# A two-block decoder kernel: latent norm summed on TensorE in small pieces, VectorE alone for the projection weights' low parts, rotary halves placed by DMA

## The reference

```python
a = h @ w_dqkv                                  # 1024 -> 384 + 256 + 32
c_q, c_kv, k_rope = split(a, [384, 384 + 256])
c_q, c_kv = rmsnorm(c_q, q_norm), rmsnorm(c_kv, kv_norm)
q = (c_q @ w_uq).reshape(B, L, 16, 96)          # 64 plain + 32 rotary per head
q = concat([q[..., :64], apply_rope(q[..., 64:], cos, sin)])
kv = (c_kv @ w_ukv).reshape(B, L, 16, 64 + 64)
k_nope, v = split(kv, [64])
k = concat([k_nope, broadcast(apply_rope(k_rope), over 16 heads)])
# causal softmax(q k^T * scale) v for each head, then @ w_o
```

## Time and profile before

| | |
|---|---|
| runs | 979.62 us median of 3 (979.53 to 981.09) |
| profiled execution | 979.78 us, of which span 978.0 us |
| PE busy | 922.1 us (94%), 7282 matmuls |
| DVE busy | 689.9 us (71%) |
| ACT busy | 517.0 us (53%) |
| POOL busy | 322.4 us (33%) |
| mean granted TensorE clock | 0.966 of full |
| DMA | 145.65 MB, mean 149 GB/s |

### The profile page before, as it was taken

The page is one execution under the profiler, slowest core; times in us unless marked ns, Lnnn a source line. Parts: engine busy times, 40 slices in busy tenths (PEclk is TensorE's granted clock), DMA queues, the critical chain, the costliest instruction groups (busy, mean ns, idle before and its releaser), DMA issues.

```text
span 978.0 us, 19924 instructions
## 1 busy us (share of the span) xinstructions
PE 922.1 (94%) x7282; PEld 895.4 (92%) x7282; DVE 689.9 (71%) x1176; ACT 517.0 (53%) x851; POOL 322.4 (33%) x225
## 2 busy tenths in 40 slices
PE   6789988999999998899999899899989999999996
PEld 6787778999998997799999899898889999999995
DVE  7457634999998225399999723779777888785666
ACT  5466655566666334656666534463346454454433
POOL 4534755000002553300000355332127334335643
PEclk9799998999999997899999999899999999999998
DMA  7322013344455352135445445253224455455431
GB/s 260 135 86 87 2 44 129 130 175 175 172 183 217 128 192 81 44 130 192 191 174 188 178 178 188 87 207 138 87 92 179 179 197 184 182 211 204 177 129 44
DMA packets 20848, 145.65 MB, mean 149 GB/s; under 512 B 2480, under 2 KB 4032, under 8 KB 5440
## 3 DMA queue, kind: packets, MB, share of 16 engines
q1 hardware_dynamic: 20800, 144.99, 40.2%
HBM read 143.94 MB, written 1.05 MB: 148 GB/s over the span
## 4 chain that ended last, share of the span: by engine, by line
PE 79%; DVE 12%; ACT 5%; issue 2%; DMA 1%; POOL 1%; SPq 0%; POOLq 0%; DVEq 0%; ACTq 0%
PE bank L409 22%; PE bank L410 22%; PE bank L411 22%; ACT w_high L832 2%; DVE w_low L1188 2%; PE bank L584 2%; PE bank L570 2%; DVE conv_out L1319 1%; PE bank L474 1%; PE bank L690 1%; PE bank L463 1%; PE bank L600 1%; DVE u_low L1197 1%; PE bank L720 1%; PE bank L458 1%
## 5 line engine op out<-in xcount | busy, mean ns | idle before, releaser
L409 PE MATMUL bank<-u_high,w_high 128*128 128x256 f32 (+2 forms) x1472 | 428.8, 291 | 25.6 <-DVE u_low L1197 16.6
L410 PE MATMUL bank<-u_low,w_high 128*128 128x256 f32 (+2 forms) x1472 | 425.2, 289 | 0.0
L411 PE MATMUL bank<-u_high,w_low 128*128 128x256 f32 (+2 forms) x1472 | 423.5, 288 | 0.0
L1682 POOL TENSOR_TENSOR w_low<-raw,w_high 128x512 fp32r<-128x512 f32 (+1 forms) x77 | 213.6, 2775 | 535.4 <-ACT w_high L832 535.4
L409 PEld LDWEIGHTS bank<-u_high,w_high 128*128 128x128 f32 x1472 | 285.1, 194 | 30.5 <-issue 11.0
L1188 DVE TENSOR_TENSOR w_low<-raw,w_high 128x1024 fp32r<-128x1024 f32 (+4 forms) x120 | 188.1, 1567 | 139.6 <-ACT w_high L832 138.4
L410 PEld LDWEIGHTS bank<-u_low,w_high 128*128 128x128 f32 x1472 | 285.0, 194 | 0.0
L411 PEld LDWEIGHTS bank<-u_high,w_low 128*128 128x128 f32 x1472 | 284.5, 193 | 0.0
L832 ACT ACTIVATE w_high<-raw 128x1024 fp32r<-128x1024 f32 (+5 forms) x120 | 197.9, 1649 | 69.9 <-PE bank L411 61.2
L409 PE MATMUL bank<-x_high,w_high 128*128 128x256 f32 (+1 forms) x608 | 174.1, 286 | 8.0 <-DVE x_low L1296 4.8
L411 PE MATMUL bank<-x_high,w_low 128*128 128x256 f32 (+1 forms) x608 | 173.9, 286 | 0.0
(11 more groups left out here) (187 smaller groups left out, 929.5 us busy)
## 6 DMA issues: line engine op xcount, KB each, us to landing
raw<-w_up_dram SPq DMA_DIRECT2D x66, 1024.0 KB, 4.8
raw<-w_down_dram SPq DMA_DIRECT2D x24, 1408.0 KB, 5.9
raw<-w_gin_c_dram SPq DMA_DIRECT2D x4, 1536.0 KB, 7.0
raw<-w_wo_dram SPq DMA_DIRECT2D x4, 1024.0 KB, 4.8
raw<-w_wout_dram SPq DMA_DIRECT2D x4, 1024.0 KB, 4.8
raw<-w_pgate_dram SPq DMA_DIRECT2D x4, 1024.0 KB, 4.7
raw<-w_gin_v_dram SPq DMA_DIRECT2D x2, 1024.0 KB, 4.7
raw<-w_gin_g_dram SPq DMA_DIRECT2D x2, 1024.0 KB, 4.7
```

The costliest lines, as they stand in the source:

```text
L409: nc.tensor.matmul(out, hi, rhi, start=start, stop=False)
L410: nc.tensor.matmul(out, hi, rlo, start=False, stop=False)
L411: return nc.tensor.matmul(out, lo, rhi, start=False, stop=stop)
L1682: nc.gpsimd.tensor_tensor(wl[n % 2][:, at], raw[n % 2][:, at], wh[n % 2][:, at].bitcast(F32), ALU.subtract).then_inc(low_parts_g, pool_cou ...
```

## The change

Five edits, all between `dkv` and the attention:

1. The squares of the five latents go to five buffers (the two of `sq` and three free blocks of `m`), so that no square waits for another. GpSimd adds nothing; TensorE sums each square over the partitions itself (`latent_sums`: an eps matmul and 15 with one column each). This stands after a quarter of `dkr`. The rows of the query latents follow one chunk later, those of the key latents two chunks after that, all inside `dkr`.
2. ScalarE makes `w_high` of `uqn` before the norm's root and not after it. VectorE makes `w_low` of `uqn` in two pieces, one for blocks 0 to 3 before the latents are multiplied and one for the rest behind them; `blocks_in_turn` waits for the second at block 4.
3. `uqn`, `uqr`, `uk`, `uv` no longer share `w_low` with GpSimd; VectorE makes all columns. The pool gains and `ropeR` go behind the latents' scaling. `low` of `uk` goes from before the first rotary group to behind it.
4. The rotary key is placed in `K` by one DMA (32 partitions, 16 copies of 272 numbers) and no longer by ScalarE.
5. The two rotary products of four heads are added at once on 128 partitions into `m`, and four DMAs place each group in `Q`. Scores wait for these DMAs.

```diff
 def pool_share(n):
-    return n == FIRST_UNIT["up0"] or UNITS[n]["name"] not in ("up0", "up1", "gin_k")
+    return n == FIRST_UNIT["up0"] or UNITS[n]["name"] not in ("uqn", "uqr", "uk", "uv", "up0", "up1", "gin_k")
...
+        latent_sq = [sq[:, 0, 0:T1], sq[:, 1, 0:T1]] + [m[:, c, :] for c in (5, 6, 7)]
...
+            def q_rope_out(q4):
+                sp.wait_ge(*done(f"q rope {q4}"))
+                for j in range(4):
+                    sp.dma_start(Q[64:96, 4 * q4 + j, :], m[32 * j:32 * j + 32, q4, :]).then_inc(q_rope_in[q4], 16)
...
+                        if name == "uk":
+                            sp.wait_ge(*done("k rope full"))
+                            sp.dma_start(K[64:96, :, :], kr[64:96, :].unsqueeze(1).to_broadcast([32, NH, T1]))\
+                                .then_inc(k_rope_in, 16)
+                        if name == "uv":
+                            q_rope_out(0)
+                        if name == "wo" and u == 0:
+                            for q4 in range(1, 4):
+                                q_rope_out(q4)
...
-            def blocks_in_turn(n, T, operands, kc):
+            def blocks_in_turn(n, T, operands, kc, first_low=None, first=0):
                 U = UNITS[n]
-                parts_ready(n)
+                if first_low is not None:
+                    pe.wait_ge(*done(first_low))
                 for b in range(U["blocks"]):
+                    if b == first:
+                        parts_ready(n)
                     bank_free(U["first"] + b)
...
-            unit(n + 2, T1, (uh, ul), None,
-                 lambda: norm_sums("c", "kv squares", squares(0, T1) + squares(1, T1),
-                                   over_what=[OVER_Q] * 3 + [OVER_KV] * 3))
-            norm_rows("c", token_rows(R_BANK, T1) + token_rows(NORM_BANK, T1, P))
+            def latent_sums():
+                sums = bank[NORM_BANK]
+                nc.tensor.matmul(sums[:, 0:6], eps_w[:, :], ones[:, 0:6], start=True, stop=False, skip_group_check=True)
+                for j in range(QC + KC):
+                    pe.wait_ge(*done(f"latent sq {j}"))
+                    what, at = (OVER_Q, 0) if j < QC else (OVER_KV, 3)
+                    for i, (t0, nt_) in enumerate(TT):
+                        last = nc.tensor.matmul(sums[0:nt_, at + i:at + i + 1], latent_sq[j][:, t0:t0 + nt_],
+                                                over[:, what:what + 1], start=False, stop=j == QC + KC - 1,
+                                                skip_group_check=True)
+                last.then_inc(*S.step("c sums"))
+            unit(n + 2, T1, (uh, ul),
+                 between={2: latent_sums, 3: lambda: norm_rows("c", token_rows(R_BANK, T1)),
+                          5: lambda: norm_rows("c", token_rows(NORM_BANK, T1, P), 3, "c rows of kv")})
...
-                pe.wait_ge(*done(f"q rope {g // 4}"))
+                pe.wait_ge(q_rope_in[g // 4], 64)
...
-            pe.wait_ge(*done("k rope"))
+            pe.wait_ge(k_rope_in, 16)
...
-                if j >= 2:
-                    act.wait_ge(*done(f"latent acc {j - 2}"))
-                nc.scalar.activation(sq[:, j % 2, 0:T1], m[:, j, :], ACT.Square).then_inc(*S.step(f"latent sq {j}"))
+                nc.scalar.activation(latent_sq[j], m[:, j, :], ACT.Square).then_inc(*S.step(f"latent sq {j}"))
+            high(n + 3)
             rms("c", 6)
-            high(n + 3)
...
-            act.wait_ge(*done("k rope full"))
-            nc.scalar.activation(K[64:96, :, :], kr[64:96, :].unsqueeze(1).to_broadcast([32, NH, T1]), ACT.Copy)\
-                .then_inc(*S.step("k rope"))
...
-                for j in range(4):
-                    part = slice(32 * j, 32 * j + 32)
-                    step = S.step(f"q rope {q4}")
-                    nc.vector.tensor_tensor(Q[64:96, 4 * q4 + j, :], ra[part, :], rb[part, :], ALU.add)\
-                        .then_inc(*step)
+                nc.vector.tensor_tensor(m[:, q4, :], ra[:, :], rb[:, :], ALU.add).then_inc(*S.step(f"q rope {q4}"))
```

More of the change, by code:

```diff
@@ L218, in program @@
         p_in = sem("p_in")
+        k_rope_in = sem("k_rope_in")
+        q_rope_in = [sem(f"q_rope_in_{i}") for i in range(4)]
         out_written = sem("out_written")
@@ L414, in weights, with unit @@
                 return wh[n % 2][:, j * P:(j + 1) * P], wl[n % 2][:, j * P:(j + 1) * P]
-            def unit(n, T, xs, chunk_ready=None, middle=None, i=None, order=None):
+            def unit(n, T, xs, chunk_ready=None, middle=None, i=None, order=None, between={}):
                 U = UNITS[n]
@@ L428, in unit @@
                         middle()
+                    if at in between:
+                        between[at]()
                     for b in range(nb):
@@ L473, in norm_rows @@
                     unit_rows = ident if name in BY_SQRT else row_ident
-                    last = nc.tensor.matmul(out, ny[:, c:c + 1].to_broadcast([P, P]), unit_rows[:, 0:out.shape[1]],
+                    last = nc.tensor.matmul(out, ny[:, first + c:first + c + 1].to_broadcast([P, P]), unit_rows[:, 0:out.shape[1]],
                                             start=True, stop=True)
-                last.then_inc(*S.step(f"{name} rows"))
+                last.then_inc(*S.step(signal or f"{name} rows"))
             def token_rows(b, n, at=0):
@@ L529, in _ @@
             unit(n + 1, T1, (uh, ul), None, lambda: norm_rows("a0", token_rows(R_BANK, T1)))
-            unit(n + 2, T1, (uh, ul), None,
-                 lambda: norm_sums("c", "kv squares", squares(0, T1) + squares(1, T1),
-                                   over_what=[OVER_Q] * 3 + [OVER_KV] * 3))
-            norm_rows("c", token_rows(R_BANK, T1) + token_rows(NORM_BANK, T1, P))
+            def latent_sums():
[12 more added lines that the diff above has]
+                          5: lambda: norm_rows("c", token_rows(NORM_BANK, T1, P), 3, "c rows of kv")})
             for k in range(QC):
                 u_ready("c")(k)
-            for name in ("uqn", "uqr"):
-                blocks_in_turn(FIRST_UNIT[name], T1, lambda b, k: (uh[:, k, :], ul[:, k, :]), QC)
+            blocks_in_turn(FIRST_UNIT["uqn"], T1, lambda b, k: (uh[:, k, :], ul[:, k, :]), QC, "uqn first low", 4)
+            blocks_in_turn(FIRST_UNIT["uqr"], T1, lambda b, k: (uh[:, k, :], ul[:, k, :]), QC)
             for k in range(QC, QC + KC):
@@ L1368, in _ @@
             keep_rows("a0", T1)
+            for j in range(QC + KC):
+                scaled(m[:, j, :], FIRST_BLOCK["dq"] + j, (freed["v"], 1), T1)
             nc.vector.tensor_tensor(psg[:, :], pcol("pool_scale", 0, 8), pcol("mix_post1", 0, 8), ALU.mult)\
@@ L1372, in _ @@
                 nc.vector.tensor_tensor(ropeR[:, hf, :], rope[:, hf, :], rows[:, :], ALU.mult).then_inc(*S.step())
-            for j in range(QC + KC):
-                scaled(m[:, j, :], FIRST_BLOCK["dq"] + j, (freed["v"], 1), T1)
             norm("c", 6)
-            low(3)
+            n = FIRST_UNIT["uqn"]
+            uqn_low, uqn_raw, uqn_high = (first_blocks(t[n % 2], QC, 4) for t in (wl, raw, wh))
+            dve.wait_ge(high_parts, n + 1)
+            nc.vector.tensor_tensor(uqn_low[0], uqn_raw[0], uqn_high[0].bitcast(F32), ALU.subtract)\
+                .then_inc(*S.step("uqn first low"))
             dve.wait_ge(*done("c rows"))
             for j in range(QC + KC + 1):
+                if j == QC:
+                    dve.wait_ge(*done("c rows of kv"))
                 if j < QC + KC:
@@ L1396, in _ @@
             low(4)
-            low(5)
             for q4 in range(4):
+                if q4 == 1:
+                    low(5)
                 b = FIRST_BLOCK["uqr"] + 2 * q4
@@ L1723, in _ @@
             low(2)
-            for j in range(QC + KC):
-                pool.wait_ge(*done(f"latent sq {j}"))
-                pool.wait_ge(*S.now())
-                step = S.step("kv squares" if j == QC + KC - 1 else f"latent acc {j}")
-                a = 0 if j < QC else 1
-                nc.gpsimd.tensor_tensor(acc[:, a, 0:T1], acc[:, a, 0:T1], sq[:, j % 2, 0:T1], ALU.add).then_inc(*step)
-            for n in range(3, 8):
-                low(n)
-            clear("c")
+            low(FIRST_UNIT["wo"])
             for g in range(NH):
```

7 lines of the change are left out of this document (6 added, 1 removed).

## The result

The changed kernel takes 968.48 us (median of 4 runs, 967.16 to 970.49) against 979.98 us (979.53 to 981.09, 4 runs) before: a ratio of 0.9883 (0.9867 to 0.9898), 11.5 us faster. Forecast were 964.1 us and a gain of 15.5. Direction, range and most of the mechanism held. The size was 4 us too good, and the clock rival's mechanism happened, at about half its price. That the range held was partly luck: the median lies 0.5 us inside its end at 969.0, and two of the four runs (969.12 and 970.49) lie outside.

What follows compares the result with a forecast made beforehand. TensorE, with 79% of the chain of waits, was taken as the bound, winnable between `dkr` and `uv`. Gain 7.4 to `uqn` plus 8.1 behind, 15.5: span 978.0 to 962.5, execution 964.3, median 964.1 us; range 962.3 to 969.0.

Steps and rivals of the forecast that it cites:

- the clock rival: Behind the sums: one-column passes bring TensorE to half clock for six microseconds, loss 2.8 us, total 967; chance 0.19.
- With the eps matmul (0.14) and 0.08 for the way back to wide matmuls: 3.0 us (2.5 to 3.6): Sums inside `dkr`: 20 passes on 128 tokens 2.24 us, ten on 16 tokens 0.56, plus these two, 3.0 us.
- The 25 ns of the Trainium skill: Sums: smallest distance of two matmuls' starts; ten short passes would take 0.25 us, the sums 2.7; not used.
- The sum by the first `uv` matmul: From `dkr` to `uv`: `uv` starts at 63.1 where it started at 78.64, gain 15.5 us.
- TensorE's own work: Up to `uqn`: `dkr` from 28.4, 6.0 us, sums 3.0, rows 1.35; done at 38.8.
- The rest: `uqn`, `uqr` and `uk`: 192 matmuls at 0.1253, 24.06 us at full clock if nothing waits.
- 3.3 are the idle times: Kernel before, `uqn` to `uv`: 32.2 us for 24.06 of matmuls, 3.3 of it idle, the rest slow clock.
- the 8.1 us: Share of the 15.5 us gain behind the start of `uqn`, up to `uv`; the other 7.4 come before.
- Does the gain reach the end?: Attention: first exponentials done near 70.3, wanted at 71.4 for the third head's scores; fits by 1.1 us.
- ScalarE and VectorE were in time: Against a rival between `dkr` and attention: one of them late, one or two microseconds come back, 966; chance 0.09.
- The key's transfer: SP queue ahead of `uv`'s load: 2.8 us by bytes; rival 21.6 by pieces; chance 0.04 for 6 to 21, 0.03 longer.
- My threshold of 6 us: SP queue: longest time the rotary key's DMA may take; each microsecond more is lost one for one.

Runs made afterwards that it cites:

- the wide filler: Kernel with the squares added up by VectorE first, plus 16 matmuls of 272 columns behind the sums, result unread; 965.45 us, ratio 0.9855.
- The fillers: Unread 2.0 us of matmuls behind the sums, in the kernel with squares added by VectorE first: nine one-column 967.17 us, or 16 wide 965.45 us.
- the norm's part: Kernel before with only sums on TensorE, early `w_high` and `w_low` of `uqn`, and no GpSimd share; 974.41 us, ratio 0.9941.
- the split kernel: Changed kernel with the sums of latents 0 to 2 one chunk of `dkr` earlier; 967.08 us, ratio 0.9866.
- the rotary part: Kernel before with only the key's DMA, one rotary addition per group with DMAs, and `low` of `uk` behind the first group; 975.01 us, ratio 0.9948.

## Why the prediction was right, and where it was not

**The step that failed** is the term "With the eps matmul (0.14) and 0.08 for the way back to wide matmuls: 3.0 us (2.5 to 3.6)", and the price of its consequence, "*The clock falls in the sums*". The sums took 33.36 - 29.90 = 3.46 us, and with the 0.10 for the way back 3.56, inside the bounds. The ten passes on 16 tokens were taken as 0.056 each, the middle between two ends and no measurement. The 30 passes took 3.32 us, 0.111 each on average, as six on 128 tokens had before: those on 16 saved nothing. Only their weight loads are shorter, as the rows of L571 show (duration least, median, longest; then the forms):

```profile
L571 PEld LDWEIGHTS bank<-mean_weights,sq x12: 92/190/192, 30.0 to 31.2; 128*128 128x128 f32 x8, 128*16 128x16 f32 x4
```

The six passes of a latent do not get shorter with it. The 25 ns of the Trainium skill (TensorE: Matmul & The Clock Gate, "Wait — 56ns, not 53.3ns?"), which I weighed and left out, are further off still as a price; the section gives them as the least distance of two starts.

**The clock rival** was given 0.19 and 2.8 us; it is what happened. All eight profiles with 3.4 us of one-column passes (of seven kernels) have the fall, behind them or, in two, already within them; the three with 1.3 us of passes, alone or with the wide filler, have none. The fillers give its price, 1.55 us. I had charged six microseconds at half clock, by the row of 35.40 to 41.00, but that fall followed idling as well; here the clock was back at 37.1, after 3.5. The six microseconds were not out of reach: in the norm's part and in the split kernel the clock stood at half for 6.9 and 6.8 us, and `uqn` came 1.4 us later still (12.35 us from the sums against 10.97), which with the 1.55 is 2.9, the rival's price.

**The sum by the first `uv` matmul.** Forecast 63.1, measured 65.03. TensorE's own work was to end at 38.8, and `uqn` started at 40.87: 0.54 for the sums (3.56 against 3.0) and 1.55 for the clock. VectorE, which was forecast to end last at 39.0, was in time, its third `u_low` ending at 39.6. The rest (24.06 forecast, 24.16 measured) held, although its 0.1253 a matmul is not quite what its row gives (15.35 over 123, 0.1248). One reading of before was short: "3.3 are the idle times" leaves out the 0.35 us at 74.09, and the earlier trace rows has 11.69 - 8.08 = 3.6. No term hangs on it, since all of the 8.1 us came back. VectorE's side was right in its rows: 1536 columns in 1.72 us, 3072 in 3.36, ending at 47.3 against a need of 50.0.

**What came behind it.** "Does the gain reach the end?" was answered yes, and through the attention it was: 13.6 at `uv`, 13.46 at 147 us. Of those, 10.7 were left in the first profile. In the second of the same program 12.9 were left, and there 0.5 us was missing at 20.64 already, ahead of the change. So of the 4.4 us by which the median missed the forecast, 1.9 are in the stage of the change, shown above, and 0.36 is that the kernel before measured higher. The other 2.1 lie further on; in the profiled execution clock falls at 303 and past 360 us make 2.3, but for the median, which has no profile, this is not shown. Those falls were in no term; the prediction took one execution of before as the rest of the program.

**The rivals that did not come.** ScalarE and VectorE were in time. For each the run with its edit undone shows what it would cost: 1.7 and 2.5 us at `uv`. The key's transfer took 6.8 us where bytes said 2.8. Part of this is company: in the rotary part, where the load of `uk` was nearly in when it was issued, it took 5.7 us, and in the nine other profiles 6.6 to 8.0. The page of the Trainium skill that I drew on (DMA: Bandwidth & Descriptors, "Why small descriptors are slow (HBM only)" and its section on the anatomy of a DMA) makes it 3.3, an estimate by that page. The trace disagrees, but that section is on DMAs that GpSimd issues, and this one was issued by SP. My threshold of 6 us was exceeded and nothing lost, for two of its parts were wrong: I let the load wait for the transfer's end, and they ran side by side, and I gave the load 7.8 us where it took 5.8. The measured slack was 6 us. What a transfer by pieces, at 21.6 us, would have done was not tried.

## What to carry to other kernels

Work that moves onto a busy TensorE as many one-column passes is priced by the pass and not by its size, and it can cost the clock besides: reduce on an engine with free time first, and leave TensorE the last step over partitions. Here VectorE's three additions, in time it had free, were worth 3.3 us in the stage and some 4 in the whole time. When an edit takes a wait away, ask what the next engine's queue holds at the new time: the two halves of this change were worth 5.6 and 5.0 us apart and 12.6 together, and with the norm's half alone ScalarE's copy became a wait of 1.17 us that was not there before. And before a microsecond or two missing from a forecast is explained, profile the same program twice.
